# A state-space mixer over blocks of four tokens, its matrices formed one feature tile at a time

## The reference

```
abar = exp(lam * dt);  bbar = (abar - 1) / lam * b          # per group and state
x[t] = abar * x[t-1] + bbar @ u[t]                          # complex, 64 states, 16 inputs
y[t] = Re(c @ x[t]) + d * u[t]
y = gelu(y);  val, gate = split(y @ w_glu);  h += val * sigmoid(gate)
```

## Time and profile before

| | |
|---|---|
| Median of three runs | 3504.86 us |
| Profiled execution, span | 3502.8 us (it is the only time shown of that execution) |
| Mean granted TensorE clock | 0.928 |
| PE busy | 3042.4 us, 87% |
| DVE busy | 2287.8 us, 65% |
| ACT busy | 935.4 us, 27% |
| POOL busy | 1537.3 us, 44% |
| HBM read | 231.58 MB, 67 GB/s |

### The profile page before, as it was taken

The page is one execution under the profiler, slowest core; times in us unless marked ns, Lnnn a source line. Parts: engine busy times, 40 slices in busy tenths (PEclk is TensorE's granted clock), DMA queues, the critical chain, the costliest instruction groups (busy, mean ns, idle before and its releaser), DMA issues.

```text
span 3502.8 us, 62449 instructions
## 1 busy us (share of the span) xinstructions
PE 3042.4 (87%) x24344; PEld 2847.5 (81%) x24344; DVE 2287.8 (65%) x3035; ACT 935.4 (27%) x1276; POOL 1537.3 (44%) x670
## 2 busy tenths in 40 slices
PE   5788899999788799989454469999999999989999
PEld 5555599999788699989444469999998988789999
DVE  5566568861677758881699975888144345478850
ACT  3122233332433233332100113333221221122221
POOL 4111055565222155555445435555643332356663
PEclk9789899999899899999677779999999999999999
DMA  3001022233111122223100002222332222112232
GB/s 110 25 27 33 19 79 84 86 107 98 60 54 48 36 73 84 84 85 103 54 1 0 0 15 89 78 87 87 112 103 77 82 67 73 55 56 89 84 104 83
DMA packets 66509, 235.52 MB, mean 67 GB/s; under 512 B 8144, under 2 KB 9040, under 8 KB 65616
## 3 DMA queue, kind: packets, MB, share of 16 engines
q1 hardware_dynamic: 63648, 225.77, 21.3%
q10 hardware_dynamic: 2736, 7.94, 0.7%
HBM read 231.58 MB, written 2.10 MB: 67 GB/s over the span
## 4 chain that ended last, share of the span: by engine, by line
PE 46%; DVE 36%; issue 13%; DVEq 2%; ACT 1%; POOL 1%; DMA 0%; ACTq 0%; POOLq 0%
PE ps L224 36%; DVE scr L426 7%; DVE scr L423 6%; DVE ub L417 4%; DVE scr L420 3%; PE ps L237 2%; DVE work L1550 2%; PE ps L245 1%; PE ps L1810 1%; DVEq L420 1%; DVE work L1046 1%; PE ps L990 1%; DVE spare L1546 1%; DVE work L792 1%; DVE scr L1538 1%
## 5 line engine op out<-in xcount | busy, mean ns | idle before, releaser
L224 PE MATMUL ps<-xs,wr 128*128 128x264 f32 x13056 | 1659.5, 288 | 71.3 <-POOL xs L336 31.6
L224 PEld LDWEIGHTS ps<-xs,wr 128*128 128x128 f32 x13056 | 1623.0, 192 | 105.0 <-issue 61.5
L212 POOL TENSOR_TENSOR wr<-raw,wr 128x1024 fp32r<-128x1024 f32 x422 | 1103.5, 2617 | 1291.0 <-ACT wr L204 1288.2
L224 PE MATMUL ps<-hid,wr 128*128 128x264 f32 x6528 | 803.4, 286 | 28.2 <-POOL wr L212 13.8
L224 PEld LDWEIGHTS ps<-hid,wr 128*128 128x128 f32 x6528 | 799.0, 190 | 32.3 <-POOL wr L212 15.6
L204 ACT ACTIVATE wr<-raw 128x1024 fp32r<-128x1024 f32 x422 | 442.1, 1050 | 442.2 <-PE ps L224 438.6
L426 DVE SCALAR_TENSOR_TENSOR scr<-ub,convp,scr 128x528 f32<-128x528 f32 x176 | 469.2, 2666 | 24.0 <-DVE scr L423 0.6
L443 DVE TENSOR_TENSOR h<-ps,h 128x528 f32 x32 | 22.7, 708 | 358.1 <-PE ps L224 357.7
L487 POOL TENSOR_TENSOR hid<-scr,hid 128x528 f32 x88 | 137.3, 1561 | 222.8 <-ACT hid L459 222.8
L423 DVE SCALAR_TENSOR_TENSOR scr<-ub,convp,scr 128x528 f32<-128x528 f32 x176 | 205.2, 1166 | 26.6 <-DVE scr L420 17.4
L1363 PE MATMUL ps<-spare,work 128*128 128x256 f32 (+1 forms) x288 | 83.5, 460 | 131.5 <-ACT spare L1618 131.2
(11 more groups left out here) (265 smaller groups left out, 2643.2 us busy)
## 6 DMA issues: line engine op xcount, KB each, us to landing
raw<-in_stream SPq DMA_DIRECT2D x422, 512.0 KB, 3.6
work<-in_ret_tab ACTq DMA_DIRECT2D x4, 1056.0 KB, 5.5
h<-in_h SPq DMA_DIRECT2D x8, 264.0 KB, 5.8
out<-h SPq DMA_DIRECT2D x8, 256.0 KB, 4.6
work<-in_s_b ACTq DMA_DIRECT2D x1, 1024.0 KB, 5.1
work<-in_s_c ACTq DMA_DIRECT2D x1, 1024.0 KB, 6.8
convp<-in_convp ACTq DMA_DIRECT2D x4, 88.0 KB, 1.9
work<-in_mla_tab ACTq DMA_DIRECT2D x1, 264.0 KB, 2.6
```

What stands on the lines that cost most here:

```text
L212: pool.tensor_tensor(wr[:, s, 1].rearrange("p a b -> p (a b)"), raw[:, s, :], wr[:, s, 0].rearrange("p a b -> p (a b)").bitcast(F32), ALU. ...
L224: mm = pe.matmul(out[:, q], wr[:, slot, w, b0 + k], x[k][v][:, q * HALF:(q + 1) * HALF], start=start and k == 0 and p == 0, stop=stop and ...
```

## The change

The mixer's stage is written anew; the FFN ahead of it gets a part of its setup; everything else stays. In words:

- **Blocks of four positions.** With C = 4 and NC = 132 blocks, the state is carried from block to block only: x[4n+4] = abar^4 x[4n] + F v, where v is the 4x16 inputs of a block, for a pair of groups 128 rows. The output of the four positions in a block is K v (products within the block, K formed from the lags) plus E x (state at the block's start). The skip d goes into K on its diagonal (`skip`).
- **Feature tile by feature tile.** The loop runs over eight feature tiles of four pairs each, over all 132 blocks at once. For each tile F is formed by `matrix` on GpSimd (`Fp`, one buffer), E on VectorE (`EP`, two buffers), each of six operations; TensorE transposes F in two halves (`ft_bank`), forms the lags (`k_bank`), the states' inputs (`V`) and the outputs (`Y`); ScalarE makes all copies: 16 blocks of 32x132 of the inputs (`U`), two halves of F (`FT`), four blocks of K (`KT`), the decay (`R`). TensorE and ScalarE do the preparation of tile t+1 ahead of the outputs and the gelu of tile t.
- **Setup.** `setup_dve` goes on after `zim` with 37 more operations on [128, 32] to [128, 160]: the powers 0 to 4 of abar, the fourth-power rotation in two squarings and a correction of its length, mag^4, and the tables of F. One more operation (`nim`) is among these 37. The rotation table of 132 columns is doubled in twelve pieces of six VectorE operations (`setup_turns`), and these come between the tails of the FFN's eight down tiles; that loop is unrolled for it. The table doubling, the two 128x1024 matrices and the transposes of the old stage go.
- **Tail of that FFN.** Since the mixer forms its inputs from h itself, scaled, high and low part are made 8 columns wide instead of 528 (`split_width`); the square and the sum stay.
- **Norm.** Its scratch is in `scr` instead of `ub`.
- **Constants.** `s5_b` and `s5_c` lose their zero halves (512 KB each instead of 1024); zeros are set by ten GpSimd memsets.

The core of the diff, with the lines taken away in the stage left out (they stand above), common indentation cut and blank lines dropped:

```diff
-S5_TILES = 2 + 2 + 6 * 8 + 4 + 2 * DT
+S5_TILES = 2 * DT
...
+unsplit = [k for k, s in enumerate(stages) if s == "s5"]
+def split_width(n):
+    return 8 if n in unsplit else T
+def split_of(n, m, i, v):
+    return scr[:, m % 2, 8 + 8 * v:16 + 8 * v].bitcast(F32R) if n in unsplit else xs[:, m + 4 * i, v]
...
-    dve.tensor_scalar(scr[:, m % 2], h[:, m + 4 * i], gains[:, first + n, bass.ds(m + 4 * i, 1)], None, ALU.mult)\
+    dve.tensor_scalar(scr[:, m % 2, 0:w], h[:, m + 4 * i, 0:w], gains[:, first + n, bass.ds(m + 4 * i, 1)], None, ALU.mult)\
...
+    def down(m, i):
+        dve.wait_ge(unit_done, ug + 3 * m + 3 + i * 12)
+        hm = h[:, m + 4 * i].rearrange("p (a b) -> p a b", a=2)
+        dve.tensor_tensor(hm, tile(gg + m), hm, ALU.add).then_inc(tile_free, 1)
+        if not last:
+            dve.wait_ge(tile_free, gg + m + 1 + i * 4)
+            tail_dve_(dve, n + 1, m, i)
+    if setup:
+        for m in range(DT):
+            down(m, 0)
+            setup[3](dve, m)
+    else:
+        with dve.Fori(0, DT // 4) as i:
+            for m in range(4):
+                down(m, i)
...
+        pe.wait_ge(c_pool.sem, c_pool.done("rz1"))
+        pe.wait_ge(tile_free, g0 + 1)
...
+        def transposes(t, c):
+            if t + c:
+                pe.wait_ge(ft_copied, 2 * t + c)
+            if c == 0:
+                pe.wait_ge(prep_f.sem, prep_f.done("f1", t))
+            for q in range(Q):
+                mm = pe.transpose(ft_bank[:, q * P:(q + 1) * P], Fp[:, c, q].rearrange("p m s -> p (m s)"), ident[:])
+            mm.then_inc(ft_pe, 1)
+        def lags(t):
+            pe.wait_ge(prep.sem, prep.done("e1", t))
+            if t:
+                pe.wait_ge(k_copied, 4 * t)
+            else:
+                pe.wait_ge(consts_in, 48)
+            for q in range(Q):
+                for c in range(2):
+                    pe.matmul(k_bank[0:32, q * P:(q + 1) * P], Fp[:, c, q, 0],
+                              EP[t % 2][:, c, q, 0:C].rearrange("p m s -> p (m s)"), start=c == 0, stop=False,
+                              tile_position=(0, 0))
+                mm = pe.matmul(k_bank[0:32, q * P:q * P + 32], ident[0:32, 0:32], skip[0:32, Q * t + q],
+                               start=False, stop=True, tile_position=(0, 0))
+            mm.then_inc(k_pe, 1)
+        def inputs(t):
+            pe.wait_ge(ft_copied, 2 * t + 2)
+            pe.wait_ge(u_copied, 16 * (t + 1))
+            if t:
+                pe.wait_ge(scan_dve.sem, scan_dve.done("ts", t - 1))
+            for c in range(2):
+                for q in range(Q):
+                    mm = pe.matmul(V[:, q, c * NC:(c + 1) * NC], FT[:, c, q], U[t % 2][:, q * NC:(q + 1) * NC],
                                    start=True, stop=True)
+            mm.then_inc(v_pe, 1)
+        def outputs(t):
+            pe.wait_ge(k_copied, 4 * (t + 1))
+            if t:
+                pe.wait_ge(gelu_made, t)
+            pe.wait_ge(scan_dve.sem, scan_dve.done("si", t))
+            for i in range(C):
+                col = (i % 2) * NC
+                for x in range(3):
+                    for q in range(Q):
+                        rows = slice(32 * q, 32 * q + 32)
+                        if x == 0:
+                            mm = pe.matmul(Y[rows, i // 2, col:col + NC], KT[t % 2][:, q, 32 * i:32 * i + 32],
+                                           U[t % 2][:, q * NC:(q + 1) * NC], start=True, stop=False,
+                                           tile_position=(0, 32 * q))
+                        else:
+                            at_ = (x - 1) * T + q * NC
+                            mm = pe.matmul(Y[rows, i // 2, col + 1:col + NC], EP[t % 2][:, x - 1, q, i + 1],
+                                           S[t % 2][:, at_:at_ + NC - 1], start=False, stop=x == 2,
+                                           tile_position=(0, 32 * q))
+            mm.then_inc(y_pe, 1)
+        def before(t):
+            transposes(t, 0)
+            lags(t)
+            transposes(t, 1)
+            inputs(t)
+        before(0)
+        for t in range(DT):
+            if t + 1 < DT:
+                before(t + 1)
+            outputs(t)
...
+    SHARE = {0: PIECES[0:3], 1: PIECES[3:5], 2: PIECES[5:7], 3: PIECES[7:9], 4: PIECES[9:11], 5: PIECES[11:12]}
+    def setup_turns(dve, m):
+        for lv, k in SHARE.get(m, ()):
+            N, at_ = (1 << lv, 1 << lv) if lv < 7 else (NC - P, P)
+            rows = NPAIR // max(1, N // 16) if lv < 7 else NPAIR
+            a_ = slice(k * rows, (k + 1) * rows)
+            t = rstd[:, 0:rows * N].rearrange("p (a b) -> p a b", b=N)
+            cN, sN = (x[:, a_, at_ - 1:at_].broadcast_to([P, rows, N]) for x in (Tc, Ts))
+            c0, s0, c1, s1 = Tc[:, a_, 0:N], Ts[:, a_, 0:N], Tc[:, a_, at_:at_ + N], Ts[:, a_, at_:at_ + N]
+            ops = ((c1, c0, cN, ALU.mult), (t, s0, sN, ALU.mult), (c1, c1, t, ALU.subtract),
+                   (s1, s0, cN, ALU.mult), (t, c0, sN, ALU.mult), (s1, s1, t, ALU.add))
+            for x, (out, in0, in1, op) in enumerate(ops):
+                dve.tensor_tensor(out, in0, in1, op).then_inc(c_dve.sem, c_dve.one(("T", lv, k, x)))
+                if x in (1, 2, 4, 5):
+                    dve.wait_ge(c_dve.sem, c_dve.done(("T", lv, k, x)))
...
+        def matrix(eng, o, t, dst, k, src, tables, names, half_a, half_b):
+            size = Q * k * 16
+            part = lambda x, c: x[:, c * size:(c + 1) * size].rearrange("p (q m s) -> p q m s", q=Q, m=k)
+            for name, out, c, src_c, tab in ((names[0], half_a, 0, 0, tables[0]), (names[1], half_a, 1, 1, tables[1]),
+                                             (names[2], half_b, 0, 1, tables[2]), (names[3], half_b, 1, 0, tables[3])):
+                eng.tensor_tensor(part(out, c), by_pair(src, t, src_c, k), by_power(tab, t, k), ALU.mult)\
+                   .then_inc(o.sem, o.one(name))
+            eng.wait_ge(o.sem, o.done(names[3], t))
+            whole = lambda x, rows: x[rows, 0:2 * size].rearrange("p (a s) -> p a s", s=16)
+            for g in range(2):
+                rows = slice(S5P * g, S5P * (g + 1))
+                eng.tensor_tensor(dst[rows].rearrange("p c q m s -> p (c q m) s")[:, :, 16 * g:16 * g + 16],
+                                  whole(half_a, rows), whole(half_b, rows), ALU.add).then_inc(o.sem, o.one(names[4 + g]))
+            eng.wait_ge(o.sem, o.done(names[5], t))
+        return matrix
...
+        def output_matrix(t):
+            if t >= 2:
+                dve.wait_ge(y_pe, t - 1)
+            matrix(dve, prep, t, EP[t % 2], C + 1, c_in, (pre, pnr, pni, pni), prep.names, half_a, half_b)
+        def inputs(t):
+            if t >= 2:
+                dve.wait_ge(u_copied, 16 * (t - 1))
+            by_chunk = lambda x: x.rearrange("p (n j) -> p j n", j=C)
+            dve.scalar_tensor_tensor(av[t % 2].rearrange("p (j n) -> p j n", j=C), by_chunk(h[:, t]),
+                                     gains[:, first + n, t:t + 1], by_chunk(rstd[:]), ALU.mult, ALU.mult)\
+               .then_inc(in_made, 1)
+        def low(t):
+            dve.wait_ge(g_act.sem, g_act.done(("hi", t)))
+            dve.tensor_tensor(hid[:, t, 1], gel, hid[:, t, 0].bitcast(F32), ALU.subtract)\
+               .then_inc(g_dve.sem, g_dve.one(("lo", t)))
+        def turn(t):
+            v = V[:, :, 0:2 * NC].rearrange("p q (c n) -> p q c n", c=2)
+            dve.wait_ge(v_pe, t + 1)
+            if t:
+                dve.wait_ge(scan_dve.sem, scan_dve.done("si", t - 1))
+            for name, out, tab in (("tc", turned, Tc), ("ts", crossed, Ts)):
+                one(scan_dve, name, dve.tensor_tensor(
+                    out.rearrange("p (c q n) -> p q c n", c=2, q=Q), v,
+                    tab[:, Q * t:Q * (t + 1)].rearrange("p q (c n) -> p q c n", c=1).broadcast_to([P, Q, 2, NC]), ALU.mult))
+        def scans(t):
+            re, im = slice(0, T), slice(T, 2 * T)
+            o = scan_dve
+            dve.wait_ge(o.sem, o.done("ts", t))
+            one(o, "wr", dve.tensor_tensor(turned[:, re], turned[:, re], crossed[:, im], ALU.add))
+            one(o, "wi", dve.tensor_tensor(turned[:, im], turned[:, im], crossed[:, re], ALU.subtract))
+            dve.wait_ge(o.sem, o.done("wi", t))
+            dve.wait_ge(decay_made, t + 1)
+            decay = R[t % 2].rearrange("p q n -> p (q n)")
+            one(o, "zr", dve.tensor_tensor_scan(turned[:, re], decay, turned[:, re], 0.0, ALU.mult, ALU.add))
+            one(o, "zi", dve.tensor_tensor_scan(turned[:, im], decay, turned[:, im], 0.0, ALU.mult, ALU.add))
+            if t >= 2:
+                dve.wait_ge(y_pe, t - 1)
+            dve.wait_ge(o.sem, o.done("zi", t))
+            both = lambda x: x.rearrange("p (c s) -> p c s", c=2)
+            tab = lambda x: x[:, Q * t:Q * (t + 1)].rearrange("p q n -> p (q n)")\
+                .rearrange("p (c s) -> p c s", c=1).broadcast_to([P, 2, T])
```

(81 more changed lines are left out.)

383 lines of the change are left out of this document (109 added, 274 removed).

## The result

The kernel after takes 3302.9 us in the median of four runs (3300.43 to 3310.21), the one before 3504.86. The ratio is 0.9425, with a 95% interval of [0.9406, 0.9443]: 5.75% faster. Forecast were 3317 and a range of 3285 to 3365. The profiled execution spans 3300.6 us at a mean granted clock of 0.938; before it were 3502.8 and 0.928.

A forecast was written before the change was run, and what follows sets the result against it. The state-space stage was taken as bound by VectorE. Its 387.5 us become 190.7, saving 196.8; less 8.9 paid in the FFN ahead, 187.9 comes off 3504.9: 3317 us, own range 3300 to 3335, given range 3285 to 3365.

The forecast's parts named there:

- norm: State-space stage's norm: 8.4 us before plus 2.8 for GpSimd's memsets and matrix beside it, 11.2 (bounds 8.4 and 14).
- FFN ahead, net: FFN before the stage: added setup and table pieces stall TensorE, shorter tail gives back 1.5; net +8.9 us.
- The wait ahead of `low`: In each tile VectorE stands idle 2.8 us after turn and inputs, until ScalarE's gelu and high part are out.
- Rival C: Products on four column groups don't run side by side; tile period 32 us, +80 to 90, total 3400; chance 0.08.
- D: GpSimd's operands in runs of 16 are slow, 20 ns a step; 49 us a tile, total 3513; chance 0.03.
- rival A: TensorE stays at 2.4 GHz and the rotation-table pieces hide in the FFN; total 3296 us; chance 0.17.
- the next V is there at X+19.0: Loop: the next tile's state inputs are ready 19.0 us after last outputs and this turn can both start.
- Scans end at X+20.8: Loop: VectorE's scans end 20.8 us after that same start, GpSimd's alternation adding 2.6; period 21.
- my own sign for it: Forecast would be wrong if the stage's VectorE isn't the last engine to finish a tile.
- a mixture: TensorE's clock in the stage varies between full and half, by the earlier mean of 0.75; used for the 21 us period.
- slow throughout: By the clock rule a tile with pauses runs at the lower clock; seven periods by 1.1, 8 us higher; not adopted.
- three more of 2.5: FFN ahead: after a first TensorE stall of 2.8 us, down tiles 5 to 7 come 2.5 us later each.

The follow-up runs named there:

- e9: Kernel after with output matrix ahead of low, added setup behind the first down tile, input products split, GpSimd's input matrix formed for the first tile only: 3272.2 us.
- e3: Kernel after with GpSimd's input matrix formed for the first tile only, the other tiles' values left out: 3301.4 us.
- e2: Kernel after with six unread TensorE products of 248 columns ahead of the lags in each tile but the first: 3297.0 us.
- e7: Kernel after with four of the eight input products issued ahead of the wait for the second transposed half of F: 3284.3 us.
- e4: Kernel after with each of the twelve rotation-table pieces in the FFN replaced by two memsets: 3304.7 us.
- e5: Kernel after with the added setup operations issued behind the first down tile's update of h instead of ahead of it: 3304.3 us.

## Why the prediction came out as it did

| step | forecast | measured |
|---|---|---|
| norm | 11.2 | 8.85 |
| to the first turn | 14.9 | 17.6 |
| first tile | 17 | 18.2 |
| second | 22.3 | 19.5 |
| five more | 105 | 102.6 |
| last tile | 20.3 | 18.3 |
| stage | 190.7 | 185.0 |
| FFN ahead, net | +8.9 | +2.1 |

**Right.** The 324 us of VectorE went, and the new prices held: scans 1.26 and 1.23, turn 2.42, output matrix 3.4, in all 14.9 us per tile (74.38 / 5 in e9) against 15.1. The order of the chain, the 16 copies at 0.33 and the side-by-side column groups were as described. The wait ahead of `low` was there, put down to ScalarE, but it took 1.3 us (line 1599 above) and not 2.8, since the outputs were shorter. Rival C is out, and D too: GpSimd's matrix took 6.0 us per tile (3.37 and 2.60 above), where 5.2 was forecast. Of rival A one half came: the pieces hid in the FFN, the clock did not stay up.

**Wrong: what ends a period.** The step that failed is "the next V is there at X+19.0" against "Scans end at X+20.8". It was the other way round: V at X+20.5, scans at X+17.5, and my own sign for it, that VectorE be the last, was not met. Both terms were mis-sized, by 1.5 up and 3.3 down, and it is luck that the later of the two came at nearly the same time in the forecast and in the run:
- GpSimd's matrix took 0.8 us of VectorE (e3: 1.07 and 1.15 back to 0.71 and 0.70), not 2.6. GpSimd did start about where I put it, 15.3 us into the period; but VectorE was ahead of my schedule, and only two of its operations were left, the sums behind `ps`. Then it waits, and the turn reads PSUM.
- The lags took 5.0 us (bounds 2 and 4, and 3 in the sum), and the input products 3.9, my upper end. Of the 2.0 that the lags were over, half is the clock and half the price: at full clock they took 3.0 (e2), not 2. With both at 1.2 GHz V is late by 1.5, although the lags began 1.2 earlier than I had it.
- The outputs took 3.2 instead of 4.4, gelu 1.11 instead of 0.63.

**The clock.** I kept a mixture, by the mean of 0.75 before. The mean of the loop is 0.67, but it isn't an even mixture. Outputs, lags and input products of the period shown above:

```profile
1816.80:1819.80 3.00, 3.00 (x97) 2.74 (x94) 3.00 (x3) 0.00 (x0) 0.78 (x1) 0.91 0.03 5
1825.90:1830.80 4.90, 4.90 (x25) 2.82 (x25) 4.76 (x5) 1.57 (x5) 0.00 (x0) 0.50 0.00 0
1833.40:1837.10 3.70, 3.70 (x16) 3.50 (x16) 0.89 (x1) 0.53 (x1) 3.55 (x5) 0.50 0.02 4
```

The lags start behind 5.38 us of idling, the input products behind 1.44, and both run at 1.2 GHz. So they do in the other tiles of the loop (lags 4.9 to 5.0 us, input products 3.8 to 3.9), but for the input products of the second period, 3.29 at a mean of 0.60. The outputs follow the input products without a gap; the clock rises in them, to a mean of 0.87 to 1.00. The Trainium skill (TensorE: Matmul & The Clock Gate, Part 1: The HAM clock gate) has the lower level as the state after idling. The trace agrees for the lags and, in most tiles, for the input products, which together are most of TensorE's share of the chain. I had weighed the rule as "slow throughout", against a mean; put to each piece by what stands ahead of it, it would have been closer: 3.8 for the input products (3.9 measured) and 4 for the lags (5.0). But the idling just ahead of a piece doesn't fix its clock. Input products behind 1.46 us ran at full clock in one tile of e3, a half of them behind 1.00 did in e7, and the lags behind the same unread products took 3.0 or 5.0 us in e2. No rule for the moment of the rise comes out of these rows.

**Wrong: the FFN.** The first stall was right (2.85 against 2.8); three more of 2.5 didn't come. The pieces were stretched as priced (up to 2.90 for an operation of 0.69), but a down tile took VectorE 17.0 us at most rather than 18.5, and TensorE ran its 792 records without a gap. e4 confirms it: nothing left to gain. The 2.1 are made up otherwise than the 8.9: from the start of the down phase to h(7) it is 118.7 us (from 1569.78) instead of 114.3 (from 1570.31), that is 4.4, of which 2.85 are the stall and most of the rest the clock behind it (from 1592 to 1595 it is 0.50 to 0.54, before the stall and from 1600 on 1.00); the end behind h(7) gave back 1.8, and the phase began 0.5 sooner.

**The norm** paid 0.4 instead of 2.8: GpSimd's ten memsets lie beside its steps, then its matrix starts as VectorE reaches its last lines.

```profile
1692.39 0.61 DVE L270 TENSOR_SCALAR scr<-scr 128x132 int32<-128x132 f32 x1
1693.04 0.30 DVE L272 SCALAR_TENSOR_TENSOR scr<-scr 128x132 f32<-128x132 f32 x1
```

```profile
1691.07 5.40 POOL L1734 MEMSET work<- 64x512 f32 x10 [1.07 <-DVE sqsum L334]
1696.74 2.49 POOL L1562 TENSOR_TENSOR work<-work,ub 128x256 f32<-128x256 f32 x4 [0.27 <-POOL work L1734]
```

The two-input steps keep their 0.30 beside the memsets. For them that is the rule of the Trainium skill (SBUF — State Buffer, SBUF: two separate sides) that I counted by, and this trace bears it out. Of the two one-input steps one was held, line 270, by about 0.4; the other kept 0.23. The last four lines didn't alternate with the matrix as I had it (1.24 us for the four, as before); 2.0 of the 2.8 were charged for nothing.

**Preparation to the first turn** took 2.7 more. The scaled inputs took 1.6 instead of 0.8, and ScalarE waited 3.5 us for the lags, 5.0 again, instead of 1.6.

The second period is 19.5 in the kernel after, shorter than the 20.5 of the rest, and 21.1 in e5. Both are the clock: in the first the outputs took 0.3 us less (2.89 at 1.00 against 3.21 at 0.89) and the input products 0.6 less, in the second the outputs 0.6 more (3.86 at 0.74). What stays open is why the clock rises where it does.

## What to carry to other kernels

When a loop passes through several engines, work out when each engine's chain delivers its piece, each at the slow end of its prices, and compare those times; two chains within 10% mean that the total is safer than the name of the bound (19.0 and 20.8 were forecast here, 20.5 and 17.5 came). An experiment that reorders the same work on the suspected engine tells busy from waiting at once, and the sign that the bound has moved is that an edit worth nothing becomes worth something. On TensorE, a product that can run inside someone else's wait saves its own time, and the clock may be up for what follows.
